# Two norms between two transformer blocks merged: the second mean taken from the first's input, tokens scaled later, context normalised earlier

## The chip, the core and the metric

The kernel runs on one core of a Trainium2 chip. PE is TensorE, ACT ScalarE, DVE VectorE, POOL GpSimd, and SP issues the weight loads. The metric is device time in microseconds (us) of one launch, as the median of several runs. TensorE's clock is either 1.2 or 2.4 GHz; the profile gives the granted share (0.50 or 1.00).

## The reference, cut to what matters

Two blocks of two layers each run one after the other: the first on 512 tokens, the second on these 512 tokens and 256 context rows, both with D = 1024. At the seam between them stand two norms in a row, and context gets one of its own:

```python
# end of the first block: l = 1 is its last layer
        h = rmsnorm(x, norm2_g[l]) * (1 + sc2) + sh2
        x = x + g2 * swiglu(h, w_ffn_in[l], w_ffn_out[l])
    return rmsnorm(x, final_g)
...
# start of the second block
        h = modulate(rms_norm(x, g_mix[l]), sa, ca)          # x is the first block's output
        hc = modulate(rms_norm(ctx, g_mix[l]), sa_c, ca_c)
        u, q, k, v = split_heads(h @ w_in[l])
        uc, qc, kc, vc = split_heads(hc @ w_in[l])
```

Here rms_norm(x, g) is x / sqrt(mean(x*x) + eps) * g over the 1024 features. The residual stream of the second block starts from rmsnorm(x, final_g).

## The kernel before

All data lie feature-major: `X` holds 8 tiles (`KT`) of 128 features by 768 columns, context in columns 0 to 255 (`TC`), tokens in 256 to 767. Every large product is done as three fp32r products (`product`, L560: high by high, low by high, high by low), so each activation tile is split into a high and a low part (`h_hi`, `h_lo`), and each weight slab is split by POOL into `weights_hi` and `weights_lo` (`gpsimd_engine`, L493) from `raw_weights`, a ring of three slabs that SP fills. The two split buffers hold two slabs; POOL starts one when PE has finished the slab before the last.

A norm is spread over four engines. ACT squares the tiles of `X` (`square`, L1190), DVE adds them up (`add_square`, L1751), PE forms the mean over features by a product with a constant matrix (`norm`, L608, its lines L613 and L617), ACT takes the root (`root`, L1198, at L1202), DVE the reciprocal (`invert`, L1761, at L1765). Then, for each tile and segment, DVE scales from `X` into PSUM (L1780), ACT rounds that to `h_hi` (L1212), DVE subtracts to get `h_lo` (L1789), and PE's first projection (`wide`, L590) takes tile after tile as they come. The squares of the next norm are taken during the last residual (`residual`, L2036, with `then`), tile by tile behind each `x<-psum,mod,x` (L2045).

Each engine has its own program, written out in order; engines meet at semaphores only. At the seam these programs say: after `feed` of layer 1, PE runs `norm(..., "final1")` and then, in `second_layer(0)`, `norm` of both segments; ACT takes the root of the first norm (L1202), squares the scaled tokens and context for the second, issues seven small DMAs, computes `lambdas(0)` (L1463), and takes two roots; DVE inverts, multiplies the tokens by g1 and the first norm's factor in place (`scale_tokens`, L2102, at L2106), adds squares of both segments, computes `lambdas(0)` (L2111) and `second_scales(0)` (L2127), waits for the axial tables, inverts twice and starts the scaling loop. `feed` (PE L861, ACT L1416, DVE L2054) is the feed-forward of a first-block layer, in three chunks of 8, 8 and 6 tiles with a down projection after each.

## Time and profile before

| | us |
|---|---|
| median of 3 runs | 3659.71 (3658.06 to 3659.78) |
| the profiled execution, as timed | 3658.79 |
| its span, from first to last instruction | 3657.3 |
| busy: PE, PE weight loads | 3456.6, 2721.0 |
| busy: POOL, DVE, ACT | 1606.9, 1333.4, 798.7 |

PE is busy 95% of the span, its granted clock averages 0.978. A row of the profile names the line of the kernel, the engine, the operation and its tiles as output<-input. A matmul in fp32 (the means) has two records. Buffer numbers are left out of names, so `h_hi` is the input of either block.

### The profile page before, as it was taken

How to read it: one execution, taken by the hardware profiler on the slowest of the kernel's cores; microseconds unless marked ns; L12 is line 12 of the kernel's file. 1: busy time of each engine (PE TensorE's matmuls, PEld its weight loads, DVE VectorE, ACT ScalarE, POOL GpSimd, SP SyncE). 2: the span in 40 equal slices, each digit the busy share in tenths (PEclk: the TensorE clock that was granted, in tenths of full speed). 3: DMA queues.
4: the chain of work that ended last, by engine and by line, in shares of the span. 5: the costliest groups of instructions: out<-in, count | busy, mean ns of one | idle time of the engine just before them, and what ended most of it. 6: DMA issues, size and time to landing. Idle time of an engine off the chain costs nothing.

```text
span 3657.3 us, 42990 instructions
## 1 busy us (share of the span) xinstructions
PE 3456.6 (95%) x17644; PEld 2721.0 (74%) x17656; DVE 1333.4 (36%) x2287; ACT 798.7 (22%) x1611; POOL 1606.9 (44%) x1020
## 2 busy tenths in 40 slices
PE   5999999999999999999999699889999989889998
PEld 3767777788877677777778587678888878667886
DVE  5843312311157433133111655651211255551113
ACT  2234411100012434111000334420100123421111
POOL 2433266566654223664566332134333333235564
PEclk7999999999999999999999899999999999999999
DMA  6344123333233441234452211022423321113321
GB/s 205 104 135 136 58 81 110 109 92 92 84 107 103 142 147 47 81 103 138 138 150 84 77 47 35 15 88 85 150 93 115 104 58 49 43 50 128 100 95 58
DMA packets 409612, 351.03 MB, mean 96 GB/s; under 512 B 9797, under 2 KB 406853, under 8 KB 409418
## 3 DMA queue, kind: packets, MB, share of 16 engines
q1 hardware_dynamic: 401568, 340.82, 30.0%
q10 hardware_dynamic: 7850, 7.47, 0.8%
q8 instruction: 141, 2.31, 0.3%
q14 instruction: 53, 0.43, 0.0%
HBM read 346.16 MB, written 2.10 MB: 95 GB/s over the span
## 4 chain that ended last, share of the span: by engine, by line
PE 88%; DVE 6%; ACT 3%; issue 1%; DMA 1%; POOL 0%; ACTq 0%; DVEq 0%; POOLq 0%
PE psum L562 26%; PE psum L563 25%; PE psum L564 25%; PE psum L544 2%; PE psum L803 2%; PE psum L911 1%; PE psum L940 1%; DVE psum L1765 1%; PE psum L793 1%; PE psum L739 1%; PE psum L631 1%; DVE k L2245 1%; PE psum L782 1%; PE psum L780 1%; PE psum L778 1%
## 5 line engine op out<-in xcount | busy, mean ns | idle before, releaser
L504 POOL TENSOR_SCALAR weights_hi<-raw_weights 128x1024 fp32r<-128x1024 f32 (+3 forms) x508 | 508.4, 1001 | 1978.6 <-PE psum L564 1745.7
L562 PE MATMUL psum<-h_hi,weights_hi 128*128 128x512 f32 (+1 forms) x2896 | 1170.0, 404 | 68.8 <-DVE h_lo L1789 53.8
L507 POOL TENSOR_TENSOR weights_lo<-raw_weights,weights_hi 128x1024 fp32r<-128x1024 f32 (+3 forms) x508 | 1107.3, 2180 | 42.4
L563 PE MATMUL psum<-h_lo,weights_hi 128*128 128x512 f32 (+1 forms) x2896 | 1101.3, 380 | 0.0
L564 PE MATMUL psum<-h_hi,weights_lo 128*128 128x512 f32 (+1 forms) x2896 | 1100.4, 380 | 0.0
L562 PEld LDWEIGHTS psum<-h_hi,weights_hi 128*128 128x128 f32 x2896 | 551.1, 190 | 232.3 <-issue 111.8
L563 PEld LDWEIGHTS psum<-h_lo,weights_hi 128*128 128x128 f32 x2896 | 552.0, 191 | 118.5 <-issue 16.8
L564 PEld LDWEIGHTS psum<-h_hi,weights_lo 128*128 128x128 f32 x2896 | 550.2, 190 | 112.9
L562 PE MATMUL psum<-hidden_hi,weights_hi 128*128 128x512 f32 (+1 forms) x1120 | 413.6, 369 | 0.0
L564 PE MATMUL psum<-hidden_hi,weights_lo 128*128 128x512 f32 (+1 forms) x1120 | 413.4, 369 | 0.0
L563 PE MATMUL psum<-hidden_lo,weights_hi 128*128 128x512 f32 (+1 forms) x1120 | 413.3, 369 | 0.0
L2045 DVE SCALAR_TENSOR_TENSOR x<-psum,mod,x 128x512 f32<-128x512 f32 (+1 forms) x184 | 123.3, 690 | 582.7 <-PE psum L564 582.5
L562 PEld LDWEIGHTS psum<-hidden_hi,weights_hi 128*128 128x128 f32 x1120 | 210.6, 188 | 40.1 <-issue 1.2
L564 PEld LDWEIGHTS psum<-hidden_hi,weights_lo 128*128 128x128 f32 x1120 | 210.8, 188 | 38.8
L563 PEld LDWEIGHTS psum<-hidden_lo,weights_hi 128*128 128x128 f32 x1120 | 210.6, 188 | 39.0
L1535 ACT ACTIVATE relu_squared<-psum 128x256 f32<-128x256 f32 (+1 forms) x96 | 47.1, 525 | 661.4 <-PE psum L564 661.4
L2158 DVE TENSOR_TENSOR psum<-psum,relu_squared 128x256 f32<-128x256 f32 (+1 forms) x96 | 58.2, 609 | 324.3 <-ACT relu_squared L1535 322.7
L544 PE MATMUL psum<-raw_weights,cond 128*32 128x256 f32 x1536 | 108.7, 405 | 25.8 <-DMA raw_weights<-in_ada_w 14.2
L1428 ACT ACTIVATE silu<-psum 128x512 f32<-128x512 f32 x44 | 26.3, 598 | 375.9 <-PE psum L564 375.9
L2059 DVE TENSOR_TENSOR silu<-psum,silu 128x512 f32<-128x512 f32 x44 | 30.4, 692 | 201.3 <-ACT silu L1428 201.3
L544 PEld LDWEIGHTS psum<-raw_weights,cond 128*32 128x32 f32 x1536 | 42.2, 113 | 76.9 <-issue 37.7
L1195 ACT ACTIVATE squares<-x 128x512 f32<-128x512 f32 x88 | 47.4, 568 | 236.1 <-DVE x L2045 216.8
(262 smaller groups left out, 3606.7 us busy)
## 6 DMA issues: line engine op xcount, KB each, us to landing
raw_weights<-in_ada_w SPq DMA_DIRECT2D x96, 1024.0 KB, 5.2
raw_weights<-in_w_mlp SPq DMA_DIRECT2D x64, 1024.0 KB, 5.4
raw_weights<-in_w_in SPq DMA_DIRECT2D x56, 1024.0 KB, 5.2
raw_weights<-in_w_ffn_in SPq DMA_DIRECT2D x88, 512.0 KB, 5.2
raw_weights<-in_w_in SPq DMA_DIRECT2D x34, 512.0 KB, 4.3
raw_weights<-in_w_out SPq DMA_DIRECT2D x16, 1024.0 KB, 5.2
raw_weights<-in_w_ffn_out SPq DMA_DIRECT2D x16, 1024.0 KB, 5.3
raw_weights<-in_w_branch SPq DMA_DIRECT2D x56, 128.0 KB, 2.2
```

Source lines behind the costliest of these rows:

```text
L504: gpsimd.tensor_scalar(whi[:, r, c0:c1], raw[:, raw_slot, c0:c1], 1.0, 1.0, ALU.mult, ALU.mult).then_inc(*split_hi.up(*key, half))
L507: gpsimd.tensor_tensor(wlo[:, r, c0:c1], raw[:, raw_slot, c0:c1], whi[:, r, c0:c1].bitcast(F32), ALU.subtract).then_inc(*split.up(*key, half))
L544: ins = tensor.matmul(bank[bk][32 * g:32 * g + 32, 0:256], cond[:, 4 * kk + g, at:at + 32], view[:, 4 * kk + g, :], start=c == 0 and kk == ...
L562: tensor.matmul(out, sh, mh, start=first, stop=False, skip_group_check=shared)
L563: tensor.matmul(out, sh, ml, start=False, stop=False, skip_group_check=shared)
L564: return tensor.matmul(out, sl, mh, start=False, stop=last, skip_group_check=shared)
L631: tensor.matmul(bank[bk][:, 0:n], matrix, x, start=True, stop=True).then_inc(*swapped.up(*key))
L803: ins = tensor.matmul(bank[3][:, i * P:i * P + P], values_of(kind, h // 2)[:, j, :], probt[:, q, j * P:j * P + P], start=j == 0, stop=j == i)
L1195: scalar.activation(part_of(work, 1 + (k + 1) % 2 if k else 0, x0, x1), X[:, k, x0:x1], ACT.Square).then_inc(*squared.up(which, l, s, k))
L1535: scalar.activation(sq2[:, count % 2, 0:c1 - c0], bank[bk][:, 0:c1 - c0], ACT.Relu).then_inc(*moved.up(L, "relu2", chunk, n, s))
L2045: vector.scalar_tensor_tensor(out=xs, in0=bank[bk][:, at:at + x1 - x0], scalar=mod[:, part * 8 + n, m:m + 1], in1=xs, op0=ALU.mult, op1=AL ...
L2158: vector.tensor_tensor(x, x, sq2[:, count % 2, 0:c1 - c0], ALU.mult).then_inc(*dve_misc.up(L, "square", count))
```

## The change

The first norm of the second block works on y = x * g1 * r1, where r1 = (mean(x*x) + eps)^(-1/2). Its mean of squares is mean((x*g1)^2) / (mean(x*x) + eps). The changed kernel therefore takes both sums, of x*x and of (x*g1)*(x*g1), while the last residual of the first block runs (`square` gets g1 as its scale for the second). With log1 = ln(mean(x*x) + eps), ACT and DVE form exp(-(ln(mean2 / exp(log1) + eps) + log1) / 2), which is r1 times the second norm's factor, and the scaling loop multiplies x by it directly, with g1 folded into the column of scales. The tokens in `X` are multiplied by g1 * r1 behind that loop (`leave`), for the residual stream. Reciprocals and roots of the two token norms are replaced by Ln and Exp (`enter_root`, `enter`). Context's squares, mean, root and reciprocal, the lambda vectors and the column scales move into the last layer's feed-forward of the first block. The loads of the second block's columns and lambda vectors are issued ahead of it; g1, those columns and lambda's columns get memory outside both blocks' own areas.

```diff
@@ -333,6 +333,9 @@
...
     small = top.take("small", [P, 16, 4])
+    gf1 = top.take("norm_g1", [P, KT])
+    lams = top.take("lambda_columns", [P, 8])
+    pcol2 = top.take("layer_columns_2", [P, 2 * KT + 4 + 1])
@@ -389,9 +391,7 @@
...
     edge = two.take("edge_factors", [P, 4, 16])
-    pcol2 = two.take("layer_columns_2", [P, 2 * KT + 4 + 1])
     lamr = cst[:, 3:5, :].rearrange("p a (b d) -> p (a b) d", d=HD)
-    lams = two.take("lambda_columns", [P, 8])
@@ -407,7 +407,10 @@
...
     ul2 = ffn2.take("hidden2_lo", [P, 8, TA], F32R)
-    work2 = Map(nc, ffn2.at).take("squares_2", [P, 3, TA])
+    sums2 = Map(nc, ffn2.at)
+    work2 = sums2.take("squares_2", [P, 3, TA])
+    roots = sums2.take("roots", [P, 2, T])
+    log1, inverse1 = roots[:, 0, :], roots[:, 1, :]
@@ -624,6 +627,23 @@
...
                 free[4], free[5] = h_lo.at(which, l, u[-2][1], u[-2][0]), h_lo.at(which, l, u[-1][1], u[-1][0])
+        def sums(which, l, s, n, bk, work, x0, x1):
+            tensor.wait_ge(*free[bk])
+            tensor.wait_ge(*paired.at(which, l, s, KT - 2))
+            tensor.matmul(bank[bk][:, 0:n], meanm, part_of(work, 0, x0, x1), start=True, stop=False)
+            tensor.wait_ge(*squared.at(which, l, s, KT - 1))
+            tensor.matmul(bank[bk][:, 0:n], meanm, part_of(work, 1, x0, x1), start=False,
+                          stop=True).then_inc(*meaned.up(which, l, s))
+        def enter(segs):
+            sums("final1", None, 0, T, 2, work1, TC, TA)
+            sums("in1", 0, 0, T, 7, work2, TC, TA)
+            free[6] = h_lo.at("in1", 0, 1, KT - 1)
+            for k in range(KT):
+                pending[k] = [h_lo.at("in1", 0, s, k) for s in range(2)]
+            free[4], free[5] = h_lo.at("in1", 0, 0, KT - 1), h_lo.at("in1", 0, 1, KT - 1)
+            free[2], free[7] = dve_misc.at("log12"), dve_misc.at("tokens", KT - 1)
...
         def swap(x, n, bk, key, matrix, ready):
@@ -873,6 +893,8 @@
...
                         next(trickle, None)
+                if l == DEPTH - 1 and t0 == CHUNKS1[-1][0]:
+                    sums("ctx1", 0, 0, TC, 6, work2, 0, TC)
@@ -1099,7 +1121,11 @@
...
-            norm([(TC, TA, TC, 1), (0, TC, 0, 2)], work2, "in1", L)
+            both = [(TC, TA, TC, 1), (0, TC, 0, 2)]
+            if L:
+                norm(both, work2, "in1", L)
+            else:
+                enter(both)
@@ -1147,7 +1173,6 @@
...
             first_layer(l)
-        norm([(TC, TA, 0, 0)], work1, "final1", None)
@@ -1192,8 +1217,9 @@
...
                     scalar.wait_ge(*paired.at(which, l, s, k - 2))
+                scale = gf1[:, k:k + 1] if (which, l, s) == ("in1", 0, 0) else 1.0
                 scalar.activation(part_of(work, 1 + (k + 1) % 2 if k else 0, x0, x1), X[:, k, x0:x1],
-                                  ACT.Square).then_inc(*squared.up(which, l, s, k))
+                                  ACT.Square, scale=scale).then_inc(*squared.up(which, l, s, k))
...
         def root(segs, which, l):
@@ -1201,8 +1227,21 @@
...
+        def enter_root():
+            scalar.wait_ge(*meaned.at("final1", None, 0))
+            scalar.activation(log1, bank[2][:, :], ACT.Ln, bias=eps[:, 0:1]).then_inc(*act_misc.up("log1"))
+            scalar.wait_ge(*act_misc.at("log1"))
+            scalar.activation(inverse1, log1, ACT.Exp, scale=-1.0).then_inc(*act_misc.up("inverse1"))
+            scalar.wait_ge(*dve_misc.at("mean2"))
+            scalar.activation(bank[7][:, :], bank[7][:, :], ACT.Ln, bias=eps[:, 0:1]).then_inc(*act_misc.up("log2"))
+            scalar.wait_ge(*dve_misc.at("log12"))
+            scalar.activation(bank[7][:, :], bank[7][:, :], ACT.Exp, scale=-0.5).then_inc(*rooted.up("in1", 0, 0))
         def norm(segs, which, l, hi):
-            root(segs, which, l)
+            if (which, l) == ("in1", 0):
+                enter_root()
+            else:
+                root(segs, which, l)
@@ -1430,6 +1469,11 @@
...
                     scalar.copy(uh[:, t - t0, :], bank[2 * q + 1][:, :]).then_inc(*hid_hi.up(l, t))
+                if l == DEPTH - 1 and t0 == CHUNKS1[1][0]:
+                    lambdas(0)
+                    scalar.wait_ge(*loaded["g1"].at())
+                    for n in range(KT):
+                        square(n, [(0, TC, 0, 2)], work2, "ctx1", 0, [loaded["ctx"].at()])
...
         def first_layer(l):
@@ -1448,10 +1492,17 @@
...
                 scalar.dma_start(X[:, :, 0:TC], a["ctx_t"].rearrange("(k p) t -> p k t", p=P)).then_inc(*loaded["ctx"].up())
+                layer_columns2(0)
             feed(l)
+            if l == DEPTH - 1:
+                scalar.wait_ge(*meaned.at("ctx1", 0, 0))
+                scalar.activation(bank[6][:, 0:TC], bank[6][:, 0:TC], ACT.Sqrt,
+                                  bias=eps[:, 0:1]).then_inc(*rooted.up("in1", 0, 1))
...
                 square(n, seg, work1, *key, [summed.at(l, "down", CHUNKS1[-1][0], n, 0)])
+                if l == DEPTH - 1:
+                    square(n, seg, work2, "in1", 0, [summed.at(l, "down", CHUNKS1[-1][0], n, 0)])
...
         def layer_columns(l):
@@ -1470,6 +1521,9 @@
...
             norm(both, "in1", L, gh)
+            if L == 0:
+                scalar.wait_ge(*scaled.at("in1", 0, 0, KT - 1))
+                scalar.activation(bank[7][:, :], log1, ACT.Exp, scale=-0.5).then_inc(*act_misc.up("rstd1"))
@@ -1693,15 +1747,9 @@
...
             first_layer(l)
-        root([(TC, TA, 0, 0)], "final1", None)
-        scalar.wait_ge(*loaded["ctx"].at())
-        for n in range(KT):
-            square(n, [(TC, TA, TC, 1), (0, TC, 0, 2)], work2, "in1", 0, [summed.at("final1", n), loaded["ctx"].at()])
...
         scalar.dma_start(gf2[:], a["g_final_cols"]).then_inc(*loaded["g2"].up())
-        layer_columns2(0)
-        lambdas(0)
@@ -1765,8 +1813,26 @@
...
+        def enter():
+            vector.wait_ge(*meaned.at("in1", 0, 0))
+            vector.wait_ge(*act_misc.at("inverse1"))
+            vector.tensor_tensor(bank[7][:, :], bank[7][:, :], inverse1, ALU.mult).then_inc(*dve_misc.up("mean2"))
+            vector.wait_ge(*act_misc.at("log2"))
+            vector.tensor_tensor(bank[7][:, :], bank[7][:, :], log1, ALU.add).then_inc(*dve_misc.up("log12"))
+            vector.wait_ge(*rooted.at("in1", 0, 0))
+        def leave():
+            vector.wait_ge(*act_misc.at("rstd1"))
+            for k in range(KT):
+                vector.scalar_tensor_tensor(out=X[:, k, TC:TA], in0=X[:, k, TC:TA], scalar=gf1[:, k:k + 1],
+                                            in1=bank[7][:, :], op0=ALU.mult,
+                                            op1=ALU.mult).then_inc(*dve_misc.up("tokens", k))
         def norm(segs, which, l, hi, lo):
-            invert(segs, which, l)
+            if (which, l) == ("in1", 0):
+                enter()
+            else:
+                invert(segs, which, l)
@@ -2045,11 +2111,12 @@
...
                                                 op1=ALU.add).then_inc(*summed.up(l, *key, n, s))
-                if then and (key != ("out2",) or n > 3):
-                    add_square(n, segs, *then)
-                if then and key == ("out2",) and n == 3:
-                    for k in range(4):
-                        add_square(k, segs, *then)
+                for sums in then:
+                    if key != ("out2",) or n > 3:
+                        add_square(n, *sums)
+                    elif n == 3:
+                        for k in range(4):
+                            add_square(k, *sums)
...
         def feed(l):
@@ -2066,13 +2133,22 @@
...
                                          ALU.subtract).then_inc(*hid_lo.up(l, t))
+                then = []
...
                     ada_finish("feed", l)
-                then = None
+                    lambdas(0)
+                    second_scales(0)
+                    then = [([(0, TC, 0, 2)], work2, "ctx1", 0)]
                 if t0 == CHUNKS1[-1][0]:
-                    then = (work1, "norm1", l + 1) if l < DEPTH - 1 else (work1, "final1", None)
+                    seg = [(TC, TA, 0, 0)]
                     if l < DEPTH - 1:
+                        then = [(seg, work1, "norm1", l + 1)]
                         first_scales(l + 1)
+                    else:
+                        then = [(seg, work1, "final1", None), (seg, work2, "in1", 0)]
+                        vector.wait_ge(*rooted.at("in1", 0, 1))
+                        vector.reciprocal(bank[6][:, 0:TC], bank[6][:, 0:TC]).then_inc(*inverted.up("in1", 0, 1))
+                        vector.wait_ge(*inverted.at("in1", 0, 1))
...
         def first_scales(l):
@@ -2128,13 +2204,19 @@
...
                 norm_scales(pcol2[:, 0:KT], 1, 0, m, ("in1", L))
+            if L == 0:
+                vector.wait_ge(*dve_misc.at("scales", "in1", 0, 2))
+                vector.wait_ge(*loaded["g1"].at())
+                vector.tensor_tensor(col[:, 0, :, 1], col[:, 0, :, 1], gf1[:], ALU.mult).then_inc(*dve_misc.up("scales_g1"))
...
         def second_layer(L):
...
             both = [(TC, TA, TC, 1), (0, TC, 0, 2)]
-            vector.wait_ge(*dve_misc.at("scales", "in1", L, 2))
+            vector.wait_ge(*dve_misc.at("scales", "in1", L, 2) if L else dve_misc.at("scales_g1"))
             norm(both, "in1", L, gh, gl)
+            if L == 0:
+                leave()
@@ -2144,7 +2226,7 @@
...
                 norm_scales(pcol2[:, KT:2 * KT], 4, 3, m, ("in2", L))
-            residual(("out2",), L, 2, outs, (work2, "in2", L))
+            residual(("out2",), L, 2, outs, [(outs, work2, "in2", L)])
@@ -2333,11 +2415,6 @@
...
             first_layer(l)
-        scale_tokens("final1", gf1)
-        for n in range(KT):
-            add_square(n, [(TC, TA, TC, 1), (0, TC, 0, 2)], work2, "in1", 0)
-        lambdas(0)
-        second_scales(0)
```

POOL and SP have the same instructions in the same order. On PE only the two products of context's mean move, from the seam to a place between the last up and the last down projection of `feed`. The instruction lists of ACT and DVE follow.

ACT before, at the seam: from the small DMAs (L1701: axial tables, L1702: last norm's g, L1460 and L1461: columns and lambda vectors) to the roots of the second norm (L1202).

```order
L1701 DMA axial_cos<-in_cos 128x512
L1701 DMA axial_sin<-in_sin 128x512
L1701 DMA constants<-in_perm 128x128
L1701 DMA edge_factors<-in_edge 128x64
L1702 DMA norm_g_107<-in_g_final_cols 128x8
L1460 DMA layer_columns_104<-in_cols 128x21
L1461 DMA constants<-in_lam 128x256
L1465 ACT_TABLE_LOAD
L1465 ACTIVATE lambda_columns<-lambda_columns 128x2
L1202 ACT_TABLE_LOAD
L1202 ACTIVATE psum<-psum,eps 128x512
L1202 ACTIVATE psum<-psum,eps 128x256
```

ACT of the changed kernel at the same place; ahead of it stand the last two squares and the DMA of the first axial table.

```order
L1751 DMA axial_sin<-in_sin 128x512
L1751 DMA constants<-in_perm 128x128
L1751 DMA edge_factors<-in_edge 128x64
L1752 DMA norm_g_107<-in_g_final_cols 128x8
L1232 ACT_TABLE_LOAD
L1232 ACTIVATE roots<-psum,eps 128x512
L1234 ACT_TABLE_LOAD
L1234 ACTIVATE roots<-roots 128x512
L1236 ACT_TABLE_LOAD
L1236 ACTIVATE psum<-psum,eps 128x512
L1238 ACT_TABLE_LOAD
L1238 ACTIVATE psum<-psum 128x512
```

Two DMAs, the lambda exponential and the second round of squares are gone from here; Ln, Exp, Ln, Exp stand in the place of the roots, each behind a table load.

DVE before, from the last add of the first norm's squares (L1758) over the last residual (L2045) to the second norm's adds:

```order
L1758 TENSOR_TENSOR squares<-squares 128x512
L2045 SCALAR_TENSOR_TENSOR x<-psum,mod,x 128x512
L1765 RECIPROCAL psum<-psum 128x512
L2106 SCALAR_TENSOR_TENSOR x<-x,norm_g_73,psum 128x512 x8
L1758 TENSOR_TENSOR squares_118<-squares_118 128x512
L1758 TENSOR_TENSOR squares_118<-squares_118 128x256
```

DVE of the changed kernel from the residual of tile 6 (L2111) to the first steps of the scaling loop (L1846, L1855):

```order
L2111 SCALAR_TENSOR_TENSOR x<-psum,mod,x 128x512
L1806 TENSOR_TENSOR squares<-squares 128x512
L1806 TENSOR_TENSOR squares_118<-squares_118 128x512
L2111 SCALAR_TENSOR_TENSOR x<-psum,mod,x 128x512
L1819 TENSOR_TENSOR psum<-psum,roots 128x512
L1821 TENSOR_TENSOR psum<-psum,roots 128x512
L1846 SCALAR_TENSOR_TENSOR psum<-x,norm_columns,psum 128x512
L1846 SCALAR_TENSOR_TENSOR psum<-x,norm_columns,psum 128x256
L1855 SCALAR_TENSOR_TENSOR h_lo<-psum,norm_columns,h_hi 128x512
```

Each residual is followed by two adds now, and between the last residual and the scaling loop stand a product and a sum where a reciprocal, eight products, twelve adds, the lambda work and two reciprocals stood.

## Rows read from the trace of the kernel before

**Rows 1.** The page's busy times: busy us (share of the span) xinstructions.

```profile
PE 3456.6 (95%) x17644; PEld 2721.0 (74%) x17656; DVE 1333.4 (36%) x2287; ACT 798.7 (22%) x1611; POOL 1606.9 (44%) x1020
```

**Rows 2.** Waits of PE: who waited for whom, total us, times, longest us.

```profile
PE psum L562 <- DVE h_lo L1789: 53.8, 11, 13.1
```

**Rows 3.** Chain of waits, 2045 to 2086: start us, us, what.

```profile
2049.08 0.76 DVE x L2045
2049.87 0.63 ACT squares L1195
2050.51 1.28 ACT L1202
2051.81 0.67 ACT psum L1202
...
2055.90 5.36 DVE x L2106 x8
2061.26 0.61 DVE squares L1758
...
2066.06 0.34 ACTq L1701
...
2068.35 0.45 ACTq L1460
2068.84 3.03 DMA constants<-in_lam
...
2080.30 0.77 DVE psum L1780
...
2083.96 0.55 PE psum L562
```

**Rows 4.** Timeline of DVE, adds of squares: start, us, operation, [idle before].

```profile
2042.17 2.69 DVE L1758 TENSOR_TENSOR squares<-squares 128x512 f32<-128x512 f32 x1 [0.70 <-ACT squares L1195]
...
2046.36 2.45 DVE L1758 TENSOR_TENSOR squares<-squares 128x512 f32<-128x512 f32 x1 [0.70 <-ACT squares L1195]
...
2939.43 3.87 DVE L1758 TENSOR_TENSOR squares<-squares 128x512 f32<-128x512 f32 x2 [0.31 <-ACT squares L1195]
```

**Rows 5.** Timeline of POOL, roundings of half a slab.

```profile
2049.13 1.04 POOL L504 TENSOR_SCALAR weights_hi<-raw_weights 128x1024 fp32r<-128x1024 f32 x1 [0.88 <-PE psum L564]
...
2941.53 1.50 POOL L504 TENSOR_SCALAR weights_hi<-raw_weights 128x1024 fp32r<-128x1024 f32 x1
```

**Rows 6.** Timeline of PE: means at two seams, and a first projection.

```profile
2048.95 1.10 PE L613 MATMUL psum<-squares,constants 128*128 128x512 f32 x2
...
2988.42 1.45 PE L613 MATMUL psum<-squares,constants 128*128 128x512 f32 x4
...
3001.28 0.77 PE L562 MATMUL psum<-h_hi,weights_hi 128*128 128x512 f32 x1 [9.63 <-DVE h_lo L1789]
```

**Rows 7.** Timeline of ACT: Exp and a table load; a sigmoid.

```profile
343.03 0.61 ACT L1283 ACTIVATE forget<-forget 5x512 f32<-5x512 f32 x1
343.65 1.28 ACT L1285 ACT_TABLE_LOAD   x1
...
1954.03 0.60 ACT L1428 ACTIVATE silu<-psum 128x512 f32<-128x512 f32 x1 [48.89 <-PE psum L564]
```

**Rows 8.** Timeline of DVE behind the scaling loop, to the first rotation.

```profile
2098.45 1.18 DVE L1789 SCALAR_TENSOR_TENSOR h_lo<-psum,norm_columns,h_hi 128x512 fp32r<-128x512 f32 x2
...
2110.21 0.70 DVE L1846 TENSOR_TENSOR psum<-psum,axial_sin 128x512 f32<-128x512 f32 x1 [7.12 <-PE psum L631]
```

**Rows 9.** Windows: us, busy us of PE, PEld, DVE, ACT, POOL, granted clock, DMA, GB/s.

```profile
2084.00:2090.00 6.00, 6.00 (x19) 5.13 (x20) 5.82 (x11) 2.94 (x6) 0.00 (x0) 0.50 0.00 0
...
3004.00:3005.00 1.00, 1.00 (x4) 0.76 (x4) 0.96 (x3) 0.48 (x1) 0.00 (x0) 0.63 0.00 0
```

**Rows 10.** DMA issues, 2060 to 2080: issues, KB each, median us to landing.

```profile
edge_factors<-in_edge ACTq DMA_DIRECT2D x1, 32.0 KB, 2.5
```

**Rows 11.** All weight loads (L486) from issue to landing.

```profile
DMA to landing us min/median/max: 2.1/5.2/13.0
```

11 lines of the change are left out of this document (5 added, 6 removed).

## The prediction

> **What bounds the kernel now.** I read the busy shares first: PE is busy 3456.6 us of the 3657.3 us span [rows 1], so only what PE executes or waits for counts. The waits of PE come next: its largest named wait is on the split input of a block's first projection, `h_lo`, 53.8 us in 11 waits, the longest 13.1 us [rows 2]. That longest one lies in the seam between the two blocks, and there I read the chain of waits [rows 3]. PE's last product of the first block lets the last residual start at 2049.08; the first product of the second block runs at 2083.96. Between them lie 34.88 us in which PE does little but three means. The chain: residual 7, its square, a table load, the root, the reciprocal, eight products with g1 (5.36 us), then a second round of squares, seven DMA issues on ACT's queue, a wait for the lambda vectors (3.03 us), table load, root, two reciprocals, and 3.66 us (2080.30 to 2083.96) from the first scaled tile to PE.
>
> **The change, part by part.**
>
> *Removed from the seam.* The reciprocals, the eight products ahead of the second round, that whole round of squares and adds, the lambda work with its two DMAs, and context's mean, root and reciprocal. All of this is on the chain of rows 3, so I don't subtract piece by piece; I rebuild the chain from 2049.08 and compare the two lengths.
>
> *Step 1, the last residual starts later: +1.6 us.* DVE now makes two adds of squares after each residual, where it made one. Such an add reads and writes SBUF, and the rows show that it doesn't run beside POOL's weight split: it took 2.69 and 2.45 us where POOL's subtraction was running [rows 4], against 0.61 us with POOL idle [rows 3]. Where two adds already follow each other, in the other block, the pair took 3.87 us [rows 4], and POOL's rounding at 2941.53 took 1.50 instead of 1.04 us [rows 5]: the first add waits for the subtraction, POOL's next instruction slips in between, and the second add waits for that. Played through for this seam: the pair of n=5, whose first add ends at 2044.86 as now, gives way to POOL once and pushes residual 6 to about 2046.4; the first add of n=6 waits for POOL's subtraction until 2048.7 and ends at 2049.3; POOL's rounding, which wants to start at 2049.13 [rows 5], goes next; the second add ends about 2050.7. Residual 7 then starts 1.6 us late. Bounds: 0 (the second add wins each time) and 3.9 (a whole locked pair ahead of it). PE has four banks, so three paces of 4.19 us (2042.17 to 2046.36 [rows 4]) of slack for the residuals before.
>
> *Step 2, residual to square: 0.79 us* (2049.08 to 2049.87) [rows 3].
>
> *Step 3, square to the first table load: 2.6 us.* Two squares take 1.3 us, but behind them ACT's queue now issues five DMAs that used to come later; five issues are 2068.35 - 2066.06 = 2.3 us [rows 3]. Bounds: 2.3 if the issues begin under the first square, 3.6 if after both. ACT's queue runs ahead of its engine by an instruction, so I stay near the lower one. PE's two means (each half of one is 1.10 us or less [rows 6]) are done before the load is. No longer ahead of the load are the two issues for the lambda vectors.
>
> *Step 4, the logarithms: 7.8 us.* As built, the kernel has four table loads, one ahead of each of Ln, Exp, Ln, Exp. From a load's start to its activation it is 1.30 us (2050.51 to 2051.81) [rows 3]; an activation of 512 columns takes 0.61 to 0.67 us [rows 3, 7]. 4 x 1.30 + 4 x 0.65 = 7.8. DVE's product and sum (0.76 us each, as a residual of that size [rows 3]) have the loads of 1.28 us beside them and cost nothing; were a load gone, its cover would go too, and each would cost that.
> None of the loads shows a pause before it: the square that starts at 2049.87 and lasts 0.63 us is followed by the load at 2050.51 [rows 3], and Exp at 343.03 by a load at 343.65 [rows 7]. The Trainium skill, "ScalarE: Activation LUTs", section "What ACT_TABLE_LOAD costs", gives each switch of sets a drain of 1.38 us beside the 1.28 us; four of those would add 5.5 us. These rows speak against it; it stays as a rival. The same page's "Table sets: the hidden batching unit" says that ln and exp share a set and need one load; the instruction order of the changed kernel shows four, so that rule isn't at work here.
>
> *Step 5, to PE: 3.7 us*, as 2080.30 to 2083.96 [rows 3]; the loop that scales and splits is the same.
>
> New seam: 1.6 + 0.8 + 2.6 + 7.8 + 3.7 = 16.5 us, against 34.9. Gain 18.4 us.
>
> *Context's mean in the feed-forward: +0.9 us.* Two means of 256 columns now run between PE's last up projection and its down projection, where PE has no gap. 512 columns took 1.10 us, 512 + 256 took 1.45 us [rows 6]: 0.35 to 0.48 each, so 0.7 to 1.0; I take 0.9. Its squares sit on ACT ahead of a sigmoid that waits 48.89 us for PE [rows 7], its adds on DVE between residuals that follow PE over those 48.89 us, eight of them, 6 us apart; the small operations for lambda and scales are there too. With a POOL lock of 2.4 us on each add they still fit. Were this cover gone, four PSUM banks would still give three residuals of slack. Root and reciprocal of context (under 3.5 us with the load) come before the first residual of the last down projection and meet the same slack.
>
> *The start of the second block: -0.8 us.* The granted clock was 0.50 (1.2 GHz) over the first 6 us of the first projection [rows 9]. In the seam of the other layer PE had idled 9.63 us, about as long as it will here (11); there the clock came back within 3004 to 3005 [rows 9], some 3.5 us after the first product at 3001.28 [rows 6]. DVE sets the other limit: eight steps from 2080.30 [rows 3] to 2099.6 [rows 8], 2.4 us each. At half clock over 6 us PE does 3 us of work less, of which DVE's pace hides about half; gain 0 to 1.6 us, I take 0.8.
>
> *Moved behind it: 0.* The eight products with g1 and an Exp now follow the last `h_lo` (2098.45 + 1.18 = 2099.6). The next that PE needs of DVE is the rotation at 2110.21, before which DVE sat idle 7.12 us [rows 8]. 5.36 us of products fit; the clearing of `pool_in` behind them may meet POOL's split and come 1 to 3 us late. The first rotated tile isn't read before the scores, behind more tiles of values and the second rotation. If this cover were gone it would cost 5.4 us at most. POOL's and SP's order is untouched, and weights for the stage are already split.
>
> **Sum.** -18.4 + 0.9 - 0.8 = -18.3 us. The profiled execution took 3658.79 us, so 3640.5; the median of before is 0.9 us above that execution, which gives 3641.
>
> **Rivals.**
> 1. *The axial tables hold DVE.* DVE's wait for these four DMAs stands ahead of its first operation of the new chain. The last of them is issued some 1.5 us after the first and landed in 2.5 us [rows 10], by my chain about 2.4 us before DVE is ready. But it now meets a 1 MB weight load, and landings of weights took up to 13.0 us [rows 11]: then the seam is 8 us longer, 3649. Chance 0.10.
> 2. *A drain at each switch*: +5.5 us, estimated from the page named in step 4, 3647. As a mechanism of this kernel it would be a pause of over 1 us before each load; two rows show none. Chance 0.05.
> 3. *DVE falls behind in the last down projection.* If each step met both locks, 1.43 (residual and square [rows 3]) + 2.69 + 1.50 + 0.61 = 6.2 us against PE's 4.19; over seven steps 14 us late instead of 1.6, 3654. Against it: the 2.69 and the 1.50 us come from one POOL slab each and fall on two different adds, and the slot without it lets DVE catch up. Chance 0.06.
> 4. *PE starts at full clock* because its idle time is shorter: 3 us less, 3638. After the wait of 9.63 us the clock was down [rows 6, 9]. Chance 0.05.
> 5. *Slower: the clock stays at half.* PE, fed at DVE's pace, would not get its clock back in the first projection. Each microsecond at half costs up to half of one, so this decides from 37 us on; held for 55 us it costs 27 less 3: 3666. Against it: it came back in both seams while DVE was feeding PE. Chance 0.02.
> Forecast itself 0.70; 0.02 for a change that is offset to within noise.
>
> **Range and chances.** The forecast's own bounds: steps 1 and 3 (-1.9, +3.3), mean (0.2), start (0.8): 3638 to 3645. To hold 8 in 10 it goes up to rival 1: 3637.5 to 3649.5. A measurement of this kernel tells 0.2%, 7 us, from no change; only rival 3 comes near (5.7 us, within) and rival 5 passes on the other side. Faster 0.93, same 0.04, slower 0.03.
>
> **What would show it.** In the changed trace: one gap of PE of 10 to 12 us in the seam, first product 16 to 17 us after the last product of the down projection; ACT with four loads of 1.28 us there; DVE's last residual over 1 us behind PE; two short means before the last down projection; no wait of PE at the first rotation. Wrong if DVE's first product waits for a DMA, if gaps stand before the loads, or if PE waits for a bank in the last down projection.

## The result: 29 us faster, ten more than forecast

The changed kernel took 3630.93 us (median of 4 runs, 3626.94 to 3631.66), the kernel before 3659.74 us beside it (3658.06 to 3661.22). The ratio is 0.9916, 95% interval 0.9901 to 0.9931: 28.8 us shorter, by the interval 25 to 36. The forecast was 3641.0 with a range from 3637.5, so the time lies below the range. The two profiled executions took 3658.79 and 3631.66 us, 27.1 us apart, with spans of 3657.3 and 3630.3 us.

**The profile after.** First the page's busy times, which answer to [rows 1]:

```profile
PE 3447.1 (95%) x17656; PEld 2726.2 (75%) x17656; DVE 1336.4 (37%) x2288; ACT 805.4 (22%) x1617; POOL 1610.1 (44%) x1020
```

PE runs the same 17656 products (12 of them are missing in the trace of before, as its weight loads show) and is busy 9.5 us less. Nothing in the forecast makes PE's own work shorter by that much: its terms were a gap that shrinks and a clock that returns earlier, for 0.8 us. This line was the first sign of the missing term.

The seam itself, in the timeline of PE (start us, us, line, operation, shape, count, [idle before and releaser]); it answers to [rows 3, 6]:

```profile
2044.38 0.39 PE L567 MATMUL psum<-hidden_hi,weights_lo 128*128 128x512 f32 x1
2045.20 1.10 PE L634 MATMUL psum<-squares,constants 128*128 128x512 f32 x2 [0.43 <-DVE squares L1806]
2047.87 1.13 PE L636 MATMUL psum<-squares,constants 128*128 128x512 f32 x2 [1.58 <-ACT squares L1221]
...
2061.05 0.55 PE L565 MATMUL psum<-h_hi,weights_hi 128*128 128x256 f32 x1 [10.34 <-DVE h_lo L1855]
```

From the start of the last product of the first block to the first of the second it is 2061.05 - 2044.38 = 16.67 us. Before it was 35.31 us: the last product started 0.43 us ahead of residual 7, and from there it was 34.88 us [rows 3]. The seam gave 18.6 us. ScalarE in the same place:

```profile
2047.19 0.63 ACT L1221 ACTIVATE squares<-x 128x512 f32<-128x512 f32 x1 [3.00 <-DVE x L2111]
2047.28 0.33 ACTq L1751 DMA_DIRECT2D axial_cos<-in_cos  x1
...
2049.09 0.45 ACTq L1752 DMA_DIRECT2D norm_g<-in_g_final_cols  x1
2049.57 1.28 ACT L1232 ACT_TABLE_LOAD   x1 [1.14 <-issue]
2050.87 0.69 ACT L1232 ACTIVATE roots<-psum,eps 128x512 f32<-128x512 f32 x1
2051.57 1.28 ACT L1234 ACT_TABLE_LOAD   x1
2052.87 0.63 ACT L1234 ACTIVATE roots<-roots 128x512 f32<-128x512 f32 x1
2053.51 1.28 ACT L1236 ACT_TABLE_LOAD   x1
...
2055.49 1.28 ACT L1238 ACT_TABLE_LOAD   x1
2056.78 0.58 ACT L1238 ACTIVATE psum<-psum 128x512 f32<-128x512 f32 x1
```

Each of the last three loads starts 0.01 to 0.02 us after the activation ahead of it ends, so there is no drain. The first one stands 1.14 us behind its square, while the queue issues the five transfers; experiment 8 takes them away, and the pause with them. And VectorE, where the last residual, the new chain and the moved products stand:

```profile
2038.10 4.15 DVE L1806 TENSOR_TENSOR squares<-squares 128x512 f32<-128x512 f32 x2 [0.70 <-ACT squares L1221]
...
2043.61 2.89 DVE L1806 TENSOR_TENSOR squares<-squares 128x512 f32<-128x512 f32 x2 [0.70 <-ACT squares L1221]
2046.42 0.74 DVE L2111 SCALAR_TENSOR_TENSOR x<-psum,mod,x 128x512 f32<-128x512 f32 x1
2053.63 0.70 DVE L1819 TENSOR_TENSOR psum<-psum,roots 128x512 f32<-128x512 f32 x1 [6.47 <-ACT roots L1234]
...
2057.40 1.15 DVE L1846 SCALAR_TENSOR_TENSOR psum<-x,norm_columns,psum 128x512 f32<-128x512 f32 x2 [1.20 <-ACT psum L1238]
...
2076.67 5.35 DVE L1827 SCALAR_TENSOR_TENSOR x<-x,norm_g,psum 128x512 f32<-128x512 f32 x8
...
2086.32 0.70 DVE L1912 TENSOR_TENSOR psum<-psum,axial_sin 128x512 f32<-128x512 f32 x1 [0.95 <-PE psum L651]
```

**Where the other ten microseconds are.** Laid beside each other, the residuals of the two kernels drift apart in stages that the change doesn't touch. At the first residual of the kernel (at 623.7 us in before) the changed one is 2.2 us behind, at the first of the last eight ahead of the seam it is 3.5 us ahead: 5.6 us gained. In the feed-forward that ends the kernel it gains another 4.8 us (from 22.2 to 27.0 us ahead). Windows of the last down projection of the first block, fully busy on both sides (us, busy us and count of PE, PEld, DVE, ACT, POOL, granted clock, DMA share, GB/s), first of before:

```profile
2018.00:2048.00 30.00, 30.00 (x131) 24.32 (x130) 15.24 (x13) 4.43 (x7) 21.70 (x15) 1.00 0.37 106
```

and of the changed kernel:

```profile
2014.00:2044.00 30.00, 30.00 (x134) 24.86 (x133) 20.62 (x19) 8.88 (x15) 22.06 (x15) 1.00 0.37 106
```

Same clock, same stage, same products, and PE did 134 of them in 30 us instead of 131. I call the time from one product's start to the next its pitch. Over all products of 512 columns that read `hidden` it was 233.0 ns before and 227.2 after (some 2585 pairs of neighbours in each trace); over those that read `h` 233.3 and 233.5. Here and below a pitch is a mean over neighbours that follow each other without a gap, outside the stretches at half clock. The name `hidden` in a trace stands for either block's tile; where the text tells them apart, `hidden2` and `h2` are those of the second block.

No instruction of these stages was changed. What the diff does to them stands in its first lines: `gf1`, `lams` and `pcol2` move to the common area, and every tile behind them starts at another SBUF address. The starts modulo 256 follow from the allocation: the weights tiles, hi and lo, are at 128 in both kernels; `hidden`, `o` and `y` went from 0 to 128, `hidden2` from 96 to 128, `h` and `h2` from 64 to 224. The tiles that came to 128 are the ones whose products of 512 columns became faster (`o` less than the others, from 232.2 to 229.4 ns).

The mean granted clock isn't the cause: it was 0.978 in the one profiled execution and 0.985 in the other, but among the four runs of the changed kernel 3631.66 us had 0.985 and 3630.9, 3630.95 and 3626.94 had 0.979 to 0.980. In the runs of experiment 1 and in those of the kernel before beside them it lies between 0.976 and 0.983 alike.

### The profile page after: what moved, and what is told of

Its sections match the earlier page's. It is cut to its first block, busy times and chain, and to the rows that moved or that the text cites. A ratio compares the mean times of both kernels' runs of the same rounds, so it can differ in the third digit from the quotient of the medians.

```text
span 3630.3 us, 43010 instructions
## 1 busy us (share of the span) xinstructions
PE 3447.1 (95%) x17656; PEld 2726.2 (75%) x17656; DVE 1336.4 (37%) x2288; ACT 805.4 (22%) x1617; POOL 1610.1 (44%) x1020
## 4 chain that ended last, share of the span: by engine, by line
PE 88%; DVE 6%; ACT 3%; issue 1%; DMA 1%; POOL 1%; ACTq 0%; DVEq 0%; POOLq 0%
PE psum L565 26%; PE psum L567 25%; PE psum L566 25%; PE psum L547 2%; PE psum L823 2%; PE psum L962 1%; PE psum L933 1%; PE psum L813 1%; PE psum L759 1%; DVE psum L1813 1%; PE psum L651 1%; DVE k L2327 1%; PE psum L802 1%; PE psum L800 1%; DMA raw_weights<-in_ada_w 1%
## 5 line engine op out<-in xcount | busy, mean ns | idle before, releaser
L565 PEld LDWEIGHTS psum<-h_hi,weights_hi 128*128 128x128 f32 x2896 | 551.2, 190 | 227.9 <-issue 107.8
L2111 DVE SCALAR_TENSOR_TENSOR x<-psum,mod,x 128x512 f32<-128x512 f32 (+1 forms) x184 | 123.3, 690 | 548.8 <-PE psum L567 548.6
L1221 ACT ACTIVATE squares<-x 128x512 f32<-128x512 f32 (+1 forms) x80 | 43.3, 563 | 248.8 <-DVE x L2111 210.1
```

The costliest lines, as they stand in the source:

```text
L565: tensor.matmul(out, sh, mh, start=first, stop=False, skip_group_check=shared)
L1221: scalar.activation(part_of(work, 1 + (k + 1) % 2 if k else 0, x0, x1), X[:, k, x0:x1], ACT.Square, scale=scale).then_inc(*squared.up(whic ...
L2111: vector.scalar_tensor_tensor(out=xs, in0=bank[bk][:, at:at + x1 - x0], scalar=mod[:, part * 8 + n, m:m + 1], in1=xs, op0=ALU.mult, op1=AL ...
```

## Experiments

Theory A: the missed part of the gain comes from the addresses. Theory B: it comes from the merged norm or from chance.

**1. The placement alone**, in the kernel before:

```
+    gf1 = top.take("norm_g1", [P, KT])
+    lams = top.take("lambda_columns", [P, 8])
+    pcol2 = top.take("layer_columns_2", [P, 2 * KT + 4 + 1])
...
-    gf1 = one.take("norm_g1", [P, KT])
...
-    pcol2 = two.take("layer_columns_2", [P, 2 * KT + 4 + 1])
-    lams = two.take("lambda_columns", [P, 8])
```

> The kernel before with one edit: the three small tensors norm_g1, lambda_columns and layer_columns_2 are allocated in the common area, as in the changed kernel, so that every activation tile behind them lies at another SBUF address (hidden, o and y from 0 to 128 modulo 256; h from 64 to 224). No instruction changes. Theory A (the part of the gain that the forecast missed comes from the start-to-start pitch of TensorE's 512-column products, which hangs on the address of the tiles read): hidden and y products go from about 233 to 227 ns, h products stay at 233 to 234, the run is 7 to 12 us shorter than before, 3648 to 3653 us. Theory B (the missed part comes from the merged norm itself or from chance between executions): pitches stay at 232 to 233 ns, the run is within 1.5 us of 3659.7.

Measured: 3650.88 us against 3659.79, ratio 0.9974 (0.9963 to 0.9984): 9.5 us by the ratio, 8.9 by the medians. `hidden` has 227.2 ns, `h` 233.5. B falls. The pitches account for it: products with `hidden` take 15.0 us less, those with `o` and `y` 2.8 less, those of 256 columns 5.7 more (`h2` 120.4 to 124.0 ns, `hidden2` 118.5 to 119.7), and those with `h` and 512 columns some 1.5 more (0.2 ns each), 10.6 in all.

**2. The change without the placement**: the changed kernel with the three tensors at the far end of SBUF.

```
-    gf1 = top.take("norm_g1", [P, KT])
+    end = Map(nc, 229216)
+    gf1 = end.take("norm_g1", [P, KT])
...
+    one.at += 32
...
+    two.at += 128
```

The two gaps keep every tile behind the three at its address of before.

> The changed kernel with one edit: the three small tensors stand at the far end of SBUF and every other tile at its address of before. Theory A: hidden and y products back at 232 to 233 ns, and what is left is the seam between the blocks: 18 to 20 us shorter than before, 3640 to 3642 us (the time forecast was 3641). Theory B: the same as the changed kernel, 3631 us, 28 to 29 us shorter than before.

Measured: 3641.77 us (3639.97 to 3642.28), ratio 0.995 (0.9938 to 0.9963): 18.0 us shorter. Pitches are back at 232.7 to 233.3 ns. This is the kernel that the forecast of 3641.0 described. With experiment 1 the parts add up, 18.0 and 9 to 10 us, to the 28.8 of the change, within the intervals. The last down projection of the first block in both (columns as in the windows above), first of experiment 1, then of this one:

```profile
2010.00:2040.00 30.00, 30.00 (x134) 24.83 (x133) 15.15 (x15) 5.01 (x8) 22.23 (x16) 1.00 0.37 106
...
2018.00:2048.00 30.00, 30.00 (x131) 24.33 (x130) 20.22 (x18) 8.31 (x15) 21.50 (x15) 1.00 0.36 106
```

With the placement alone PE does 134 products in 30 us. With the merged norm alone, and with its added squares on DVE and ACT, it does 131, as before.

**3 and 4. Bytes left free** behind the common tensors of the kernel before, `top.at += 64` and `top.at += 128`; nothing else.

> The kernel before with 64 bytes left free behind the common tensors: h and h2 go from 64 to 128 modulo 256, hidden, o and y from 0 to 64, hidden2 from 96 to 160. No instruction changes. Theory A in its sharper form (the short pitch belongs to a start of 128 modulo 256, where the weights tiles start too): the 512-column products of h in both blocks, some 6500 of them, go from 233 to 227 ns, those of hidden stay at 232 to 233, and the run is 30 to 40 us shorter, 3620 to 3630 us. A weaker form (the pitch hangs on the address, but by another rule): some stage moves by over 3 ns, none has to be h. Theory B: no stage moves by more than 1 ns, 3659.7 us within 1.5.

> The kernel before with 128 bytes left free: hidden, o and y at 128 modulo 256 as in the changed kernel, h and h2 at 192, hidden2 at 224. Theory A in its sharper form: products of hidden in the first block, of o and y 227 ns; h, h2 and hidden2 at 232 to 235 ns; 6 to 9 us shorter than before. Weaker form: hidden as said, h and hidden2 anywhere from 226 to 236. Theory B: no change.

Measured: 3630.66 us (ratio 0.9921, 0.9908 to 0.9935), 0.7 us above the range expected, and 3627.24 us (0.9913, 0.9900 to 0.9927). 64 bytes left free were worth as much as the whole change. In the first, `h` and `h2`, now at 128, had 227.9 and 228.5 ns, `hidden` 233.3. In the second `hidden` had 226.9 and, against my expectation of 232 to 235 for `h`, `h` at 192 had 229.3 and `h2` 229.7; the 6 to 9 us expected were 32.5. So 128 isn't the only good start.

**5. The weights moved too**: `top.at += 128` ahead of the weights tiles. Everything behind them stands as in experiment 4; only the weights' start differs, 0 instead of 128.

> The kernel before with 128 bytes left free ahead of the weights tiles: weights go from 128 to 0 modulo 256, everything behind them as in the kernel with 128 bytes left free behind the common tensors (h and h2 192, hidden, o and y 128, hidden2 224). A1 (the start of the activation tile decides): pitches as there, hidden 227 ns, h 229, and 3627 us within 2. A2 (the distance decides): the distances are those of the kernel before except for h (192 against 192, so the same too), every pitch is as before, 232 to 233 ns, and the time 3660 us within 3. A3 makes no statement on the pitches by itself.

Measured: 3661.66 us against 3660.88, ratio 1.0003 (0.9994 to 1.0012), and every pitch as before (`h` 233.3, `hidden` 232.5). All of experiment 4's 32.5 us (by the medians) are gone with `h` and `hidden` at the very same addresses. The same stage in experiment 4 and in this one:

```profile
1993.00:2023.00 30.00, 30.00 (x134) 24.81 (x133) 15.78 (x14) 4.43 (x7) 22.31 (x15) 1.00 0.37 106
...
2018.00:2048.00 30.00, 30.00 (x131) 24.32 (x130) 15.00 (x13) 4.43 (x7) 21.70 (x15) 1.00 0.36 106
```

What counts is the distance from the weights tile to the activation tile, modulo 256 (distance from here on).

**6. Products alone.** A kernel with no other work: per placement 32 triples, 96 products in all, each with its weight load. All its tiles are filled with zeros.

```
tensor.matmul(out, wh[:, k, c:c + P], hh[:, k, 0:n], start=k == 0, stop=False)
tensor.matmul(out, wh[:, k, c:c + P], hl[:, k, 0:n], start=False, stop=False)
tensor.matmul(out, wl[:, k, c:c + P], hh[:, k, 0:n], start=False, stop=k == KT - 1)
```

> A kernel of products alone (the reference's computation is left out): 96 three-term products of 512 columns, with the weights tile and the activation tile each at a chosen start, one choice after another, first with TensorE alone, then with copies running on VectorE, ScalarE and GpSimd. Theory A1 (the pitch belongs to the reading of the activation tile alone): already alone, with weights at 128 modulo 256, about 227 ns for an activation start of 128, 229 for 192, 232 to 235 for 0, 32, 64, 96, 160 and 224; with weights at 0 the same starts are short. Theory A2 (it belongs to the distance between weights and activation): with weights at 0 the short start is 0, with weights at 64 it is 64. Theory A3 (it is the meeting of TensorE's reads with other engines' accesses): alone all starts within 1 ns of each other, and a difference of some 6 ns only in the second part.

Five windows of 20 us of its trace (columns as above): weights at 128 and the activation at 96, 128 and 192; then weights at 0 and the activation at 0 and 32.

```profile
112.00:132.00 20.00, 20.00 (x87) 16.14 (x86) 0.00 (x0) 0.00 (x0) 0.00 (x0) 1.00 0.00 1
134.00:154.00 20.00, 20.00 (x90) 16.55 (x89) 0.00 (x0) 0.00 (x0) 0.00 (x0) 1.00 0.00 0
...
178.30:198.30 20.00, 20.00 (x89) 16.39 (x88) 0.00 (x0) 0.00 (x0) 0.00 (x0) 1.00 0.00 1
267.00:287.00 20.00, 20.00 (x90) 16.58 (x89) 0.00 (x0) 0.00 (x0) 0.00 (x0) 1.00 0.00 1
289.00:309.00 20.00, 20.00 (x88) 16.05 (x87) 0.00 (x0) 0.00 (x0) 0.00 (x0) 1.00 0.00 1
```

Full clock throughout, no other engine, no transfer, and still 90 products at distance 0 against 87 or 88. Mean pitches of 512 columns: distance 0 226.7 to 226.9 ns, with weights at 128, 0 and 64 alike; 64 229.0; the other six between 232.3 and 234.3. With copies beside the products each of the eight distances had the same pitch as alone, within 0.2 ns. The copies ran out on the way, however: GpSimd's ended at 691.9 us of the trace, ScalarE's at 741.7, VectorE's at 816.4. So all three engines were at work for the distances 128, 160 and 192, ScalarE and VectorE for 224 and 0, and VectorE alone for most of 32 and for 64 and 96. A1 falls with distance 0 at three starts of the weights, A3 with the differences that are there with PE alone; A2 stands. For 256 columns the order is another one: distance 192 has 113.4 ns, distance 0 119.9.

**7. The best placement**, from the map of 6: `h`, `hidden`, `o`, `y` and `hidden2` at distance 0, `h2`, which is read with both widths, at 64. First in the kernel before, then in the changed one; the edit shown is that of the changed one. In the kernel before the gaps are 64 bytes ahead of `h`, 64 behind the first block's small tensors and 128 ahead of `h2`, and the rest is the same.

```
-    pcol2 = top.take("layer_columns_2", [P, 2 * KT + 4 + 1])
+    pcol2 = Map(nc, 229248).take("layer_columns_2", [P, 2 * KT + 4 + 1])
...
-    identb = one.take("identity_bf16", [P, P], BF16)
-    causal = one.take("causal_bf16", [P, P], BF16)
     hh = one.take("h_hi", [P, KT, T], F32R)
     hl = one.take("h_lo", [P, KT, T], F32R)
+    identb = one.take("identity_bf16", [P, P], BF16)
+    causal = one.take("causal_bf16", [P, P], BF16)
...
+    one.at += 96
...
+    two.at += 64
...
+    two.at += 32
```

> The kernel before with its tiles laid so that h, hidden, o, y and hidden2 lie at distance 0 from the weights modulo 256 and h2 at 64 (two small bf16 tensors behind h, one small tensor at the far end, gaps filled). No instruction changes. By the pitches measured so far: h 4318 products x 5.5 ns, hidden 1053 x 5.9, o and y 2.8 us, h2 2240 x 3.6, less 256-column products 2.8, plus 1.5 for those that move weights, hidden2 1533 x 5.8 less 0.9: 46.6 us shorter than before, 3614 us, between 3609 and 3620. Rival: the stages meet another bound (VectorE, GpSimd's rounding, the transfers) once the products are shorter, and less than 38 us is gained.

> The changed kernel with the same placement. If seam and placement add up: 46.6 us of placement in all and 18 us of seam, 3595 us, 3590 to 3600; 35 us shorter than the changed kernel. Rival: another bound takes over, 3600 us or more.

Measured: 3610.18 us (ratio 0.9871, 0.9858 to 0.9885) and 3593.13 us (3592.01 to 3595.39; ratio 0.9821, 0.9808 to 0.9835), against 3658.71 beside them. 48.5 us of placement where 46.6 were worked out, and 65.6 in all, so 17.1 for the seam, where experiment 2 had 18.0: seam and placement add. No other bound took over. This version beats both kernels, the changed one by 37.8 us by the medians of the two sessions and by 35 us by the ratios. Its busy times:

```profile
PE 3406.9 (95%) x17644; PEld 2720.6 (76%) x17656; DVE 1336.8 (37%) x2288; ACT 805.9 (22%) x1617; POOL 1611.2 (45%) x1020
```

The share of busy time is 94 or 95%, here as in the other versions: it can't show this loss, since the page counts PE as busy while its products are slow.

**8. The five small transfers behind the roots**, in the changed kernel and in the best one. They stood between the last squares and the first table load.

```
             scalar.activation(bank[7][:, :], bank[7][:, :], ACT.Exp, scale=-0.5).then_inc(*rooted.up("in1", 0, 0))
+            for dst, name in ((cos2, "cos2"), (sin2, "sin2"), (perm2, "perm2"), (edge, "edge")):
+                scalar.dma_start(dst[:], a[name]).then_inc(*loaded["axial"].up())
+            scalar.dma_start(gf2[:], a["g_final_cols"]).then_inc(*loaded["g2"].up())
...
-        for dst, name in ((cos2, "cos2"), (sin2, "sin2"), (perm2, "perm2"), (edge, "edge")):
-            scalar.dma_start(dst[:], a[name]).then_inc(*loaded["axial"].up())
-        scalar.dma_start(gf2[:], a["g_final_cols"]).then_inc(*loaded["g2"].up())
...
             if L == 0:
                 leave()
+                vector.wait_ge(*loaded["axial"].at())
...
-        vector.wait_ge(*loaded["axial"].at())
```

> The changed kernel with the five small transfers for the second block issued behind the last of the four root steps instead of ahead of the first table load. By the chain of the changed kernel the first load then starts right behind ScalarE's last squares, 1.1 us sooner, and TensorE's gap shrinks from 16.4 to 15.3 us: 1.1 us shorter than the changed kernel, 3629.8 us where that has 3630.9. Rival: VectorE, which waits for these transfers ahead of the first rotation, has the tables late (issue at 2057, landing 3 to 4 us later, rotation at 2086: nothing), or TensorE's means end later than the load, in which case less than 0.3 us is gained.

> The changed kernel with the placement and with the five small transfers behind the root steps: 0.7 us shorter in TensorE's gap at the seam than with the placement alone, as in the run without the placement, so within 1 us of it in time; a difference of more than 2 us either way would say that something else follows from the move.

The timeline of ScalarE in the first of them:

```profile
2047.53 0.71 ACT L1221 ACTIVATE squares<-x,norm_g 128x512 f32<-128x512 f32 x1
2048.25 1.28 ACT L1232 ACT_TABLE_LOAD   x1
...
2057.24 1.05 ACT L1254 ACTIVATE h_hi<-psum,norm_columns 128x512 fp32r<-128x512 f32 x2 [1.20 <-DVE psum L1846]
```

The pause of 1.14 us ahead of the first load is gone. The stretch from PE's last product of the first block to its first of the second, however, went only from 16.67 to 15.93 us, 0.74 shorter. The other 0.4 us were lost again at the end of the chain: VectorE's first scaled tile was ready at 2056.84 (2056.07 and 0.77 us), but ScalarE's queue issued transfers until 2057.20, and `h_hi` started at 2057.24. In time this is not to be seen: 3631.68 us (ratio 0.9921, 0.9908 to 0.9935) and 3592.72 us (0.9821, 0.9807 to 0.9834). Inconclusive by the clock, shown by the trace alone.

**9. Finer steps, and a miss.** A second kernel of products alone, with steps of 16 bytes and with hi and lo apart.

> Products alone again (the reference's computation is left out), TensorE alone, with finer steps of the distance from the weights tile's start to the activation tile's (modulo 256), and with the two halves of a pair at different starts. D1 (the distance between the addresses read at the same time decides, product by product): where only weights lo is moved, only one or two of the three products of a triple change, by the distance of the pair that they read; between distance 0 (227 ns) and 64 (229) the pitch of 512 columns rises and falls in steps, with its top of 232 to 235 at odd places. D2 (the start of the tiles counts as a whole): all three products of a triple have the same pitch in every case. With both weights at 128 and distance 0 the pitch is 227 and 120 ns for 512 and 256 columns again, with distance 192 233 and 113.

Neither as put. With weights lo alone at another start, two of the three products of a triple slowed (227.5, 232.4 and 234.0 ns), which speaks for D1; but at distances 64 to 112 the three differed (226.0, 229.1 and 231.7 ns at 64) though all had one distance. One more place had 226.7 ns, distance 240, and 256 columns had 117.2 there. I took that into the whole kernel, with `h2` at distance 240. Against the best placement:

```
+    stat2 = two.take("softmax_stats_2", [P, 4, 8])
+    gf2 = two.take("norm_g2", [P, KT])
...
     two.at += 64
-    gh = two.take("h2_hi", [P, KT, TA], F32R)
-    gl = two.take("h2_lo", [P, KT, TA], F32R)
+    h2 = two.take("h2", [P, 2 * KT * TA + 8], F32R)
+    gh, gl = (h2[:, 4 + KT * TA * n:4 + KT * TA * (n + 1)].rearrange("p (k t) -> p k t", k=KT) for n in (0, 1))
...
-    stat2 = two.take("softmax_stats_2", [P, 4, 8])
-    gf2 = two.take("norm_g2", [P, KT])
-    two.at += 32
```

> The kernel of the placement alone with h2 at distance 240 instead of 64 from the weights (modulo 256), every other tile as there. If the map of the kernels of products alone holds in this kernel to its finer steps: the 512-column products of h2, 2240 of them, go from 229.5 to 227.5 ns (4.5 us), its 256-column products, 1311 with h2 moving, from 118.6 to 117.4 (1.6 us), and the products that move weights keep 116 (their distance is then 16, measured 113.3, against 192, 113.5): 6 us shorter, 3587 us, where the placement alone had 3593. If the map holds only at steps of 32: pitches between 229 and 233, no gain or a loss of up to 8 us.

Measured: 3602.38 us (ratio 0.9845, 0.9832 to 0.9859), 9 us longer than the best placement, not 6 shorter: `h2` 233.5 ns instead of 229.6. So I asked the products alone again, first for a longer period or the layout of rows, then for repetition.

> Products alone (the reference's computation is left out), TensorE alone, weights at 128. It asks why distance 240 had 226.7 ns in the second kernel of products and 233.3 in the whole kernel with h2 there. M1 (the period of the pattern is longer than 256: the start there was 16 below the weights modulo 512, in the whole kernel 240 above): the start 112 has 227 ns, the start 368 some 233, with the rows of both layouts, while 128, 384 and 640 stay alike. M2 (the layout of the rows decides: weights rows of 256 columns, activation rows of 768 tokens, 24576 bytes from hi to lo): 112 and 368 are alike within 1 ns for rows of 512, and both long with one of the other row lengths. M3 (something else in the whole kernel): 227 ns for both in every layout.

> Products alone (the reference's computation is left out), TensorE alone, 512 columns, weights at 128, sixteen activation starts in steps of 16 three times over in shuffled order, and the start 112 (distance 240) six more times. It had 226.7 ns once and 233.3 in all other places. N1 (at some distances the two reads can settle in more than one pattern, by what ran before): distance 0 has 227 ns and distance 64 has 229 every time, while 240 and some others spread over 3 ns or more from one time to the next. N2 (each distance has its one pitch): every distance repeats within 1 ns, and 240 has either 227 or 233 in all nine.

The first of these had 233.3 ns at distance 240 in every layout, 16 bytes below the weights or 240 above, modulo 512 (236.6 at two starts further up); one of these cases has the very addresses that had shown 226.7. M1 and M3 fall with that, and M2 doesn't explain it either, since the row length changed nothing. The second has the answer in two stretches with identical addresses (weights at 128, activation at 112). The timeline of PE in the first:

```profile
71.45 0.39 PE L47 MATMUL psum<-h,weights 128*128 128x512 f32 x1
...
73.04 0.39 PE L45 MATMUL psum<-h,weights 128*128 128x512 f32 x1
```

and in the second:

```profile
249.52 0.39 PE L47 MATMUL psum<-h,weights 128*128 128x512 f32 x1
...
251.15 0.39 PE L45 MATMUL psum<-h,weights 128*128 128x512 f32 x1
```

Between the two rows shown lie seven pitches each time: 1.59 us, so 227 ns, and 1.63 us, so 233 ns. Over eight stretches of this kernel distance 240 had 226.7 twice, 233.3 four times and 236.4 to 236.7 twice; distances 176 and 208 also had two values (231.1 and 233.3, 230.0 and 234.7), and 112 had 231.1 in one kernel and 226.7 in another. N1 stands: at some distances the stream settles in one of several patterns. Distance 0, by contrast, had 226.7 to 227.6 ns in all its 17 stretches of 512 columns in the four kernels, and distance 64 229.0 to 229.1 in all 10.

## Why the prediction was wrong, point by point

- *Step 1, last residual 1.6 us late*: right. It starts 2.04 us after the last product of the down projection, before 0.43: 1.61 us. The locked pair of adds ahead of residual 6 took 4.15 us (forecast from 3.87), the pair ahead of the last residual 2.89. PE waited for no bank.
- *Step 2*: 0.77 us (0.79). *Step 3*: 2047.19 to 2049.57, 2.38 us (2.6). *Step 4*: 2049.57 to 2057.40, 7.83 us (7.8). *Step 5*: 2057.40 to 2061.05, 3.65 us (3.7). Sum 16.24, forecast 16.5.
- *Context's means*: two pairs of 0.59 us, from 2011.06 to 2012.08, about 0.9 us on PE (0.9). *Start of the second block*: from the first product some 3.2 us at 0.50 of full clock instead of 6 [rows 9]; the first projection took 18.5 us instead of 19.5, so 1.0 us (0.8).
- *Moved products*: 5.35 us, and VectorE then still waited 0.95 us for PE at the first rotation, where it had waited 7.12 [rows 8]. Hidden, with 1 us left of that cover.
- *Rivals*: none came true. 1 (tables late): VectorE's wait ends with ScalarE's roots, not with a transfer. 2 (drain): the last three loads start within 0.02 us of the activation before them, against the drain of 1.38 us in the Trainium skill, "ScalarE: Activation LUTs", section "What ACT_TABLE_LOAD costs"; the pause of 1.14 us ahead of the first load is the five issues of step 3. 3 (VectorE behind): its last residual is 1.6 us late, not 14. 4 and 5 (clock): it was at 0.50 for some 3.2 us and at 1.00 from 2065 on, so neither full at once nor low for long.

The clock at the start of the second block, in windows of the changed kernel (columns as in those of the result):

```profile
2061.00:2064.00 3.00, 2.95 (x10) 2.69 (x11) 2.93 (x6) 1.57 (x4) 0.00 (x0) 0.50 0.00 0
2064.00:2065.00 1.00, 1.00 (x6) 0.81 (x6) 0.96 (x2) 0.31 (x1) 0.00 (x0) 0.90 0.08 16
2065.00:2066.00 1.00, 1.00 (x8) 0.86 (x7) 0.96 (x3) 0.69 (x1) 0.00 (x0) 1.00 0.00 0
```

So the mechanism and its sizes were right: this part measured 18.0 us alone, forecast 18.3. **What failed is the account of the change.** "The change, part by part" goes through what is removed, added and moved among instructions, and has no term for the three allocations that stand first in the diff. They moved the twelve tiles that PE reads in three quarters of its products; that was worth 9.5 us alone (experiment 1) and 10.8 us on top of the seam (3641.77 to 3630.93), and it made the range's lower end wrong, since no bound in it was for that term. It can't have been priced from the trace of before alone, where all distances of that kernel (128, 192 and 224) are of the slow kind; but that the addresses changed could be read from the diff, and a bound from both sides put beside it. That `hidden`, `o`, `y` and `hidden2` came to distance 0 was luck: nobody had chosen their new places.

## What to carry to other kernels

An edit of the allocation is an edit of the time: when tiles move, compare the pitch of unchanged stages, from one start to the next, before anything is credited to the change itself; busy shares don't show it. Where a kernel is bound by fp32r products of 512 columns, put the activation tiles at the same start modulo 256 as the weights tiles; here such a placement, with `h2`, which is read with both widths, at distance 64, was worth 48 us of 3659 with not one instruction changed. For 256 columns another distance is the good one, and other data types weren't measured here. And of a placement that looked good once, ask for a repetition: distance 0 held everywhere, distance 240 did not.

## What the runs showed of the hardware

- The pitch of fp32r products with their weight loads depends on the distance between the starts of the two operands in SBUF. At the granted clock of 1.00, 512 columns: 226.7 ns at distance 0, 229.0 at 64, 230 to 238 at most others (the highest, 238.0, at distance 4; 226.7 in some stretches at 112 and 240); 256 columns: 113.4 at 192, 119.9 at 0. The Trainium skill, "TensorE: Matmul & The Clock Gate", section "Back-to-back issue gap", has N / 2.4 + 2.5 ns for an isolated product, 215.8 for 512 columns, and about 131 ns for a stream of weight loads and products of that width, neither with a term for an address. No stretch of 512 columns here came below 226 ns.
- It needs no other engine: the differences are there with PE alone, and copies on one to three engines changed no pitch by more than 0.2 ns (experiment 6). The Trainium skill, "SBUF — State Buffer", section "A bandwidth-pool intuition that's wrong (but worth ruling out)", has contention as structural only, by a port lock or a starved descriptor generator; here PE's product stream alone gains or loses 3% by addresses.
- Moving the weights alone, with the activations at rest, took away the whole gain (experiment 5). That the reads of a weight load and of the product beside it meet in the same part of the memory would fit this, but it is argued, not shown; no run separated the weight load from the product.
- Some distances have two or three stable pitches at one and the same pair of addresses. What chooses between them stays open.
